# Second MLP of a two-block transformer kernel: the second product of six rounds from seven products of halves

## The reference, cut to what matters

```
u = x * (1.0 + scale) + shift
y = jnp.square(jax.nn.relu(u @ mlp_w1[layer] + mlp_b1[layer])) @ mlp_w2[layer] + mlp_b2[layer]
x = layer_norm(ALPHA * x + gate * y, ln_g[layer, 1], ln_b[layer, 1])
```

## Time and profile before

| | us |
|---|---|
| median of 3 runs | 3797.22 (3795.74 to 3801.22) |
| the profiled execution | 3808.3 |
| its span | 3806.2 |
| PE busy | 3672.5 (96%) |
| DVE, ACT, POOL busy | 1904.4, 1195.8, 1685.2 |

### The profile page before, as it was taken

One profiled execution on the slowest core, in us unless ns is written; L12 is line 12 of the kernel. 1 busy time (PEld: TensorE's weight loads), 2 busy tenths in 40 slices (PEclk: granted clock), 3 DMA queues, 4 the chain that ended last, 5 costly groups with the idle time before them and its releaser, 6 DMA issues.

```text
span 3806.2 us, 49998 instructions
## 1 busy us (share of the span) xinstructions
PE 3672.5 (96%) x18117; PEld 2979.8 (78%) x18117; DVE 1904.4 (50%) x3250; ACT 1195.8 (31%) x1931; POOL 1685.2 (44%) x1782
## 2 busy tenths in 40 slices
PE   6999999999999899999989999999998999999997
PEld 5778878888887677777767888888787778888886
DVE  6863364333344465665575222223598564444445
ACT  5422241111113555555543111111315332222223
POOL 2542276555552422222228654444463284444342
PEclk9999999999999999999999999999999999999999
DMA  7421013233320011111111211111121111111121
GB/s 232 124 72 35 29 39 111 88 94 94 94 83 23 26 43 45 40 45 48 32 36 49 63 52 50 44 44 44 30 65 45 31 47 50 50 44 55 39 72 44
DMA packets 247642, 223.52 MB, mean 59 GB/s; under 512 B 12586, under 2 KB 194488, under 8 KB 247497
## 3 DMA queue, kind: packets, MB, share of 16 engines
q1 hardware_dynamic: 221440, 170.04, 14.8%
q10 hardware_dynamic: 26057, 51.52, 4.3%
HBM read 217.27 MB, written 4.26 MB: 58 GB/s over the span
## 4 chain that ended last, share of the span: by engine, by line
PE 61%; DVE 3%; ACT 2%; issue 1%; DVEq 0%; ACTq 0%
PE PS L726 8%; PE PS L727 8%; PE PS L728 8%; PE PS L1147 3%; PE PS L867 3%; PE PS L869 3%; PE PS L868 3%; PE PS L1148 3%; PE PS L1149 3%; PE PS L753 3%; PE PS L755 3%; PE PS L754 3%; PE PS L1193 2%; PE PS L1226 2%; PE PS L1207 2%; PE PS L1349 1%
## 5 line engine op out<-in xcount | busy, mean ns | idle before, releaser
L726 PE MATMUL PS<-UH,WH 128*128 128x512 f32 (+1 forms) x2192 | 867.6, 396 | 14.2 <-DVE UL L2326 5.1
L728 PE MATMUL PS<-UH,WL 128*128 128x512 f32 (+1 forms) x2192 | 859.9, 392 | 0.0
L727 PE MATMUL PS<-UL,WH 128*128 128x512 f32 (+1 forms) x2192 | 859.6, 392 | 0.0
L3362 POOL TENSOR_TENSOR WL<-RAW,WH 128x256 fp32r<-128x256 f32 x1001 | 842.5, 872 | 21.0
L3359 POOL TENSOR_SCALAR WH<-RAW 128x1024 fp32r<-128x1024 f32 x251 | 276.1, 1100 | 1288.9 <-PE PS L728 468.4
L726 PEld LDWEIGHTS PS<-UH,WH 128*128 128x128 f32 (+1 forms) x2192 | 414.2, 189 | 108.7 <-DVE UL L2326 7.6
L728 PEld LDWEIGHTS PS<-UH,WL 128*128 128x128 f32 (+1 forms) x2192 | 413.7, 189 | 89.2
L727 PEld LDWEIGHTS PS<-UL,WH 128*128 128x128 f32 (+1 forms) x2192 | 414.3, 189 | 85.7 <-issue 0.2
L2258 DVE TENSOR_TENSOR X<-PS,X 128x512 f32<-128x512 f32 x416 | 281.3, 687 | 392.6 <-PE PS L869 384.0
L1793 ACT ACTIVATE SQ<-PS,PV 128x512 f32<-128x512 f32 x128 | 88.2, 689 | 1016.0 <-PE PS L728 987.6
L867 PE MATMUL PS<-WH,HH 128*128 128x512 f32 x1024 | 401.2, 392 | 4.7 <-DVE HL L2670 4.7
(11 more groups left out here) (377 smaller groups left out, 5966.7 us busy)
## 6 DMA issues: line engine op xcount, KB each, us to landing
RAW<-in_mlp_w_dram SPq DMA_DIRECT2D x128, 512.0 KB, 3.9
ADM<-in_ada_w_dram ACTq DMA_DIRECT2D x96, 256.0 KB, 3.4
RAW<-in_w_up_dram SPq DMA_DIRECT2D x44, 512.0 KB, 3.9
ADR<-in_ada_w_dram ACTq DMA_DIRECT2D x32, 512.0 KB, 4.1
WR<-in_od_w_in_dram SPq DMA_DIRECT2D x32, 512.0 KB, 4.3
RAW<-in_w_down_dram SPq DMA_DIRECT2D x22, 512.0 KB, 3.3
RAW<-in_ev_w_in_dram SPq DMA_DIRECT2D x20, 512.0 KB, 3.9
RAW<-in_w_in_dram SPq DMA_DIRECT2D x20, 512.0 KB, 3.9
```

The costliest lines, as they stand in the source:

```text
L726: pe.matmul(bank(b)[0:width], wh, xh, start=(k == 0), stop=False)
L727: pe.matmul(bank(b)[0:width], wh, xl, start=False, stop=False)
L728: mm = pe.matmul(bank(b)[0:width], wl, xh, start=False, stop=(k == NK - 1))
L3362: ins = pool.tensor_tensor(WL[slot][:, c], r[:, c], WH[slot][:, c].bitcast(F32), ALU.subtract)
```

## The change

The six rounds of the loop become twelve of 256 hidden columns (`ROUNDS_S = 12`), for the second MLP alone. In each, the hidden activations of the round are a 2 x 2 matrix of quarters (2 blocks of 128 columns `m` x 2 halves of tokens `h`), the rows of w2 are a 2 x 2 matrix of quarters of 128 x 512 (b11, b12, b21, b22), and the product is made of seven products of sums of such quarters, in the form of Strassen and Winograd. One product is 4 token blocks x 3 matmuls, each a bank of its own (28 banks a round); DVE adds each to a quarter of `X` or to one of three accumulators `ACC1`, `ACC5`, `ACC6` (128 x 2048 each). Each accumulator belongs to several quarters of `X` and is added to them once, after the last round (`merge`). PE does the `up` products of round s + 1 with the products of round s between their steps of contraction. The first `up` products have no partner, and the last products are done between those of the final old round, two at a step.

PE and the order of the products:

```diff
+SUMS_AT = {0: "s1", 2: 2, 3: "s3", 5: 3, 6: "s2", 8: 4, 9: "s4", 11: 5, 13: 6, 21: 0, 26: 1}
+RING = (0, 1, 2, 3, 0, 1, 2)
+                def groups(first, n):
+                    def between(k):
+                        if k < 7:
+                            for i in range(n):
+                                group(first + n * k + i)
+                    return between
+                for m, h in QUARTERS:
+                    up(m, h)
+                with rounds(pe, ROUNDS_S - 1, (w1, 2), (a_free, 4), (d_free, 28), (wc, 7), (hc, 7)):
+                    for i, (m, h) in enumerate(QUARTERS):
+                        up(m, h, groups(7 * i, 1))
+                for i in range(2):
+                    last_up(i, groups(14 * i, 2))
```

ACT:

```diff
+                src = (HR[0], HR[2], SUMH, HR[1], HR[0], SUMH, HR[3])
+                def relu(q, b1):
+                    up.take()
+                    settle()
+                    turn[0] += 1
+                    r = HR[q][:, :]
+                    free(act.activation(r, bank((turn[0] - 1) % NA), ACT.Relu, bias=b1))
+                    mine.wait_at(0)
+                    act.activation(r, r, ACT.Square).then_inc(S("st_h"), 1)
+                def sums_and_rest():
+                    for j in (2, 3, 4, 5, 6):
+                        if j >= 4:
+                            prod.wait_at(4 * (j - 3))
+                        if j < 6:
+                            sums.take()
+                        settle()
+                        high_h(j)
+                        if j != 5:
+                            wt.take()
+                        high_w(j)
+                def next_half_tile(b):
+                    relu(0, bias(b))
+                    relu(1, bias(b))
+                    wt.take()
+                    prod.wait_at(20)
+                    settle()
+                    high_w(0)
+                    high_h(0)
+                    relu(2, bias(b + 1))
+                    wt.take()
+                    prod.wait_at(24)
+                    mine_h.wait_at(0)
+                    settle()
+                    high_h(1)
+                    high_w(1)
```

```diff
+                def s1():
+                    hr.take(4)
+                    sum_(SUMH, HR[1], HR[3], ALU.add)
+                def s3():
+                    own.wait_at(0)
+                    sum_(HR[1], HR[0], HR[1], ALU.subtract)
+                def s2():
+                    own.wait_at(0)
+                    sum_(HR[0], SUMH, HR[0], ALU.subtract)
+                def s4():
+                    own.wait_at(0)
+                    sum_(SUMH, HR[2], HR[0], ALU.subtract)
+                def final(i):
+                    if SUMS_AT.get(i) not in (0, 1):
+                        regular(i)
+                    if i == 15:
+                        merge(X21, X22)
+                    if i == 19:
+                        merge(X11, ACC1)
+                        merge(ACC6[:, :, :], ACC1, "st_merge")
+                for a in (ACC1, ACC5, ACC6):
+                    dve.memset(a[:, :, :], 0.0)
+                mine.wait_at(0)
+                chain.done(dve.tensor_tensor(X21, X21, X22, ALU.subtract))
 ...
+                    merge(X12, ACC5)
+                    merge(X22, ACC5, "st_merge")
+                    low(0)
+                    low(1)
+                    merge(X12, ACC6)
+                    merge(X21, ACC6)
+                    merge(X22, ACC6, "st_merge")
+                    low(2)
+                    low(3)
+                    add_x(BY_COLUMN[0])
                     ln_vectors(4, None, ALPHA_2, pv("b_out_2", 0, NK))
                     ln_vectors(5, None, ALPHA_2)
+                    stats(0, 1)
+                    stats(2, 3)
```

```diff
+                def combinations(column_1):
+                    diff(t, b12, b11)
+                    column_1()
+                    diff(b12, b22, b12)
+                    low(2)
+                    diff(t, b22, t)
+                    low(3)
+                    low(4)
+                    low(5)
+                    diff(t, b21, t)
+                    low(6)
+                def second_column():
+                    up.wait_at(4)
+                    column(1)
+                def next_rows():
+                    gate(0)
+                    gate(1)
+                    low(0)
+                    low(1)
+                column(0)
+                column(1)
+                next_rows()
+                up.wait_at(2)
+                column(0)
+                with rounds(pool, ROUNDS_S - 2, ...
+                    combinations(second_column)
+                    up.wait_at(6)
+                    column(0)
+                    next_rows()
```

More of the change, by code:

```diff
@@ L896, in mlp @@
                     pe.wait_ge(S("t_free"), T_AT["u", 1, 1, 7] + 1)
[L897 to L911, removed]
-                    pe.wait_ge(S("mod_ready"), 5)
+                    with rounds(pe, 6, (w_ready, 8), (a_free, 8), (d_free, 16), (h_ready, 8), (ada_sum, 2)) as it:
+                        for h in range(2):
+                            for i in range(4):
+                                up(i, h)
+                            for g in range(2):
+                                down(BY_COLUMN[h][4 * g:4 * g + 4], h, g == 0, 1 - h)
+                                if g == 0:
+                                    columns(it, h)
+                    for i in range(4):
+                        up(i, 0)
+                    w_ready.take(4)
+                    down(BY_BLOCK[0][0:4], 0, True)
+                    down(BY_BLOCK[0][4:8], 0, False)
+                    pe.wait_ge(S("mod_ready"), 5)
+                else:
+                    seven_products(lambda i, between: up(i, 0, between=between))
+                    up(2, 0)
+                    up(3, 0)
+                    down(BY_COLUMN[0][0:4], 0, True, 1)
+                    down(BY_COLUMN[0][4:8], 0, False, 1)
                 up(0, 1)
@@ L2662, in _, with merge, seven_products, sum_ @@
             hh_ready = Tally(dve, S("hh_ready"))
+            X11, X12, X21, X22 = (X[:, 4 * i:4 * i + 4, half(j)] for i, j in QUARTERS)
+            def merge(x, y, signal=None, op=ALU.add):
+                mine.wait_at(0)
+                chain.done(dve.tensor_tensor(x, x, y if y is X22 else y[:, :, :], op))
+                if signal is not None:
+                    dve.sem_inc(S(signal), 1)
+            def seven_products():
+                prod, hh, hr = Tally(dve, S("st_prod")), Tally(dve, S("st_hhi")), Tally(dve, S("st_h"))
+                own = Tally(dve, S("st_s"))
+                src = (HR[0], HR[2], SUMH, HR[1], HR[0], SUMH, HR[3])
+                into = (ACC1, X11, ACC5, X22, ACC6, X12, X21)
+                def sum_(out, a, b, op):
+                    dve.tensor_tensor(out[:, :], a[:, :], b[:, :], op).then_inc(S("st_s"), 1)
+                    own.skip()
+                def low(j):
+                    hh.take()
+                    r = RING[j]
+                    dve.tensor_tensor(HCL[r][:, :], src[j][:, :], HCH[r][:, :].bitcast(F32), ALU.subtract)\
+                        .then_inc(S("st_hc"), 1)
+                def s1():
[10 more added lines that the diff above has]
+                    sum_(SUMH, HR[2], HR[0], ALU.subtract)
+                steps = {"s1": s1, "s2": s2, "s3": s3, "s4": s4}
+                def products(after):
+                    for i in range(28):
+                        prod.take()
+                        turn[0] += 1
+                        x = into[i // 4][:, i % 4, :]
+                        free(dve.tensor_tensor(x, bank(NA + (turn[0] - 1) % ND), x, ALU.add))
+                        after(i)
+                def regular(i):
+                    f = SUMS_AT.get(i)
+                    if f in steps:
+                        steps[f]()
+                    elif f is not None:
+                        low(f)
+                def final(i):
[8 more added lines that the diff above has]
+                    dve.memset(a[:, :, :], 0.0)
+                mine.wait_at(0)
+                chain.done(dve.tensor_tensor(X21, X21, X22, ALU.subtract))
+                low(0)
+                low(1)
+                with rounds(dve, ROUNDS_S - 1, (prod, 28), (mine, 28), (hh, 7), (hr, 4), (own, 4)):
+                    products(regular)
+                products(final)
@@ L2699, in mlp @@
                 add_x(BY_COLUMN[1])
[L2700 to L2705, removed]
+                if l == 0:
+                    with rounds(dve, 6, (gd, 24), (mine, 16), (hh_ready, 8), (ada_in[0], 128), (ada_in[1], 128),
+                                (ada_step, 16)):
+                        for h in range(2):
+                            gd.skip(4)
+                            for i in range(4):
+                                low(i)
                                 ada_steps(h, [2 * i, 2 * i + 1])
-                        add_x(BY_COLUMN[h])
+                            add_x(BY_COLUMN[h])
+                else:
```

(5 more changed lines are left out.)

250 lines of the change are left out of this document (209 added, 41 removed).

## The result

The changed kernel takes 3807.1 us (median of 19 runs, 3796.9 to 3816.2) where the kernel before, run beside it, takes 3798.9 (19 runs): a ratio of 1.0021, 95% interval 1.0013 to 1.0029, so 5 to 11 us slower. The forecast was slower, by 27 us. So I compare the stage alone, from the start of PE's gap of 3.59 us ahead of it to the start of the gap of 1.89 us behind it. It takes 759.4 us, before 753.1. "Late" is counted from where a matmul would have started at the steady pace, a "gap" is what the profile shows in brackets; a gap of 1.40 is a start 1.56 late.

A forecast was written before the change was run, and what follows sets the result against it. TensorE was taken as the bound, busy 96% of the span. Terms: -32.6 + 26.4 + 14.0 + 5 + 13 + 1.5 = +27.3 us on the median 3797.2, so 3825 us; range 3784 to 3848.

The forecast's parts named there:

- the sign: Whole kernel: slower than before; slower by more than 7.6 us was given a chance of 0.70.
- the removed matmuls: Second MLP's rounds: twelve fewer matmuls, twelve times, 144 x 0.2267 us, -32.6 us.
- rival 4: Second MLP: down products still take 96 matmuls' time, for their signals and waits; 3857 us or more; chance 0.02.
- the whole path of the wait in the round: Steady round: s4, `high_w(5)`, POOL's `low(5)` and difference, `high_w(6)`, `relu(0)`, then PE; 11 rounds.
- the entry: Round 0: PE waits 3.4 us for POOL's `column(0)`, plus 1.7 of slow clock; +5 us (3.4 to 5.5).
- the exit: Behind the last products: statistics of the first four blocks, 12.3 us beside 10.9 of two `up`; +1.5 us (0 to 3).
- the moved loads: w2 rows and w1 columns, issued over 10 us ahead: 0; paired loads of the first modulation: 0 (-0.3 to +1).
- the total of the tail: Last products and final old round: PE late for DVE, +10 us, and +3 for two slow stretches; 5 to 26.
- the term of the stall: Each of 11 rounds: PE waits 2.4 us for ACT's `relu(0)`, +26.4 us; 1.2 from below, 3.3 from above.
- the term of the clock: Behind the rounds' stalls: three in four of 11 followed by slow clock, losing 1.7 us each; +14.0 us (0 to 18.7).
- rival 2: The rounds' stall is there but PE's clock holds: +9 us, 3806 us; chance 0.18.
- rival 1: The rounds' chain is short: stall 1.2 us, under every gap followed by slow clock; -10 us, 3787; chance 0.22.

The follow-up runs named there:

- one more copy: The changed kernel with one more ACT copy of 128 x 512 between `high_w(6)` and `relu(0)` of each round; 3833.5 us (1 run).

## Why the prediction was right and wrong

Right: the sign; the removed matmuls at 0.2267 us each, with no loss for their signals (rival 4); the place, the number and the whole path of the wait in the round; the entry (3.4 and 1.7 forecast, 3.1 measured; the clock held there in this profile and fell in five of the seven that have this wait); the exit, 1.5 and 1.1; that the moved loads cost nothing (PE waits for no load from the first new product on).

Right by luck: the total of the tail, 10 + 3 forecast, 11.3 + 2.0 measured. I had 7.4 for DVE's additions, sums and merges; it was 3.4, since eight of the nine sums took 0.67 to 0.73 us, not 1.13, and the three merges 2.29, 2.73 and 2.71, not 2.8. DVE's last remainders were over when forecast (56.2, measured 56.4 us behind the tail's start at 2582.0), but by two errors that cancel: the products were done sooner, and the five late merges took 17.3 us and not 14. And I looked at the last of POOL's weight tiles alone and put the others at nothing: the first and the second w2 tile made PE late by 1.87 and 5.58, and the second of these waits hid the one for DVE. The sign owes something to luck too: with the two sizes below put right my own sum is +6, less than the 7.6 us that I called no change.

Wrong: the time. The step that failed is the term of the stall, 2.4 us a round, which measured 1.56 of late start, 1.73 with the slower first matmuls behind it; and with it, the larger error, the term of the clock, 14.0, which measured 0. Followed along the chain, with the round's start at 2199.2: s4 was over at 15.8 and not 16.15, since the sums and remainders of DVE before it met POOL less often than I had them (`low(4)` took 0.85, s2 0.67, where I had 1.2 each): 0.37 less. ACT took 0.11 and not 0.20 from s4 to `high_h(5)`: 0.09 less. POOL's `low(5)` took 1.97 and not 1.85, and started 0.04 later behind ACT and handed over 0.04 later: 0.20 more. POOL's difference took its 1.44 us alone, because DVE's `low(6)` came only as it ended (2219.73), where I had both at once and 1.8: 0.36 less. From the difference to the end of relu it was 1.24 and not 1.5: 0.26 less; a `settle` in front of relu seems to cost nothing there, behind a busy ACT. PE started 0.05 behind relu, which I had not counted. Together some 0.83 less. I had added contention at every sum whose neighbour was busy on average, and the rounds have both in step: each meeting has to be placed on both timelines.

The price of the clock was near, but it was put on a gap that did not come. Three of the four gaps of 2.02 to 2.66 us were followed by a slow stretch; with one more copy, at 2.28 us, it is 7 of 11 (2.53 in the first). In the changed kernel, ten gaps of 1.40 and one of 1.72, it is none of 11. My stall of 2.4 would have been shown as a gap of 2.2, where the price holds; the real one lies below. Where between the two sizes it begins, no run here shows. So 26.4 + 14.0 had to be 19.0 + 0. With the rest of the sum unchanged that gives +6, where +8.2 was measured: nearest to rival 2 in time (+9), but by rival 1's condition, a stall under 2 us, without its faster end. I gave no case the middle, 1.7.

The ports hardly mattered where I weighed them, in the chain: from `low(4)` to relu only `low(5)`, 1.97 us for two pieces that take 1.44 alone, and `low(4)`, 0.85 for 0.69, were longer. They mattered in the tail. POOL's gate ran from 2616.03 to 2618.43; the merge issued at 2616.26 ended at 2620.57, 4.31 us long and 2.14 behind the gate's end. Where the merge was first, at 2600.54, it took 2.29, and POOL's piece issued at 2601.33 took 2.10 instead of 0.74. And while POOL's four pieces of a w1 tile (from 2605.23 on) and DVE's next two merges alternated, a merge took 2.7 and a piece beside it 2.8. The Trainium skill (SBUF — State Buffer, Terms) has VectorE and GpSimd take the shared pair of ports in turn, each for a whole instruction. The trace agrees: the merge of 4.31, the piece of 2.10 and the first merge of 2.7 are each as long as the rest of the other's instruction and their own time together, less some 0.15 us.

## What to carry to other kernels

Removing work from the bounding engine pays only as far as what it hands to others comes back in time. Here one order decided it: an instruction that frees a bank of the bounding engine stood behind one that waits for a third engine, and moving it ahead turned 0.2% slower into 0.35% faster. When a short stall repeats in a loop, settle its size before the clock behind it is priced: here a gap of 1.4 us cost itself, and one of 2.3 itself and up to 1.1 us a round of clock on top. When a tail is added up, every tile that the bounding engine will take needs its time, not the last one alone. Large elementwise instructions of two engines that held each other up here belong in different stretches.

## What the runs showed of the hardware

- Gaps of TensorE in otherwise unbroken matmuls: of 1.40 us none of 30 (three kernels) was followed by a lower clock; of 2.28 us 6 of 10, of 2.91 6 of 10, of 4.18 all 10, the stretches 3.4 or 6.8 us long at granted clock 0.50, and at 2.91 in the repeated order none, 6.8, 3.4.
- A DVE sum of two 128 x 2048 SBUF tiles took 2.29 us where it came before POOL's instruction, and 2.7 to 4.4 where it came behind one; POOL's four pieces of 256 columns took 2.8 alone and 6.9 to 7.7 beside such sums.
- DVE's additions from PSUM took 0.68 to 0.70 us in all 336 of the changed stage, POOL busy or not.
